# Attention's projection started with the token-by-token unit, between the transposes of the two token tiles

## The chip, the cores and the metric

The kernel runs on one core of one Trainium2 chip. The metric is the device time of one execution in microseconds (us); lower is better. Times are the median of several executions; the rows of the profile come from one profiled execution.

## What is computed

The reference is a network of two blocks, each with two layers, on 256 tokens of width 1024, in float32. Each layer of the first block is a SwiGLU feed-forward, an attention mixer, and a second feed-forward. The change is in the attention mixer, of which this is the part that matters:

```python
proj = h @ w_in                      # h = rms_norm(x), 256 x 1024
q_n, kv_n, gate_n, moba = jnp.split(proj, [...], axis=-1)
# kv_n: k_cmp, v_cmp, k_slc, v_slc, k_win, v_win of two key/value heads
kc = compress(k_cmp, pos_ck, w_ck1, w_ck2)     # gelu(flat(blocks + pos) @ w1) @ w2
vc = compress(v_cmp, pos_cv, w_cv1, w_cv2)
q_rot, k_slc, k_win = (apply_partial_rope(t, cos, sin) for t in (q, k_slc, k_win))
# three branches of scores, softmax and sum, weighted by sigmoid(gate_n);
# beside them eight heads of a second attention (moba), then  @ w_out
```

## The kernel before

The program is written by hand, engine by engine: each phase has a function for SyncE (`sync`, which issues all loads), ScalarE (`scalar`), VectorE (`vector`) and TensorE (`tensor`), and their order is the order of the code. Engines meet only at semaphores. The mixer's phase is `nsa_phase`; it runs twice, once per layer, each time after a feed-forward phase.

**Numbers in two parts.** A float32 product is made of three matmuls of `fp32r` parts (`matmul3`, lines 88 to 90): each operand is split into a high part, which ScalarE writes (`activation ... Copy`), and a low part, which VectorE writes (value minus high). That holds for weights and for activations.

**The norm and the transposes.** The tokens are two tiles of 128 (t = 0, 1). Per tile, ScalarE squares and sums two halves (`norm_scalar`), VectorE adds, inverts and scales (`norm_vector`), TensorE transposes in blocks of four (`turn_block`: block b is half b % 2 of tile b // 2, in bank b), ScalarE copies each block's high part (`turned_high_scalar`) and VectorE makes its low part (`turned_low_vector`). Between the blocks TensorE runs matmuls whose result is not used (`keep_clock(n)`; each of the n is two rows of the trace).

**The ring of weight units.** The projection's weight comes in 12 units of 256 columns, one of them of 280 (the values of two branches and the gate logits). A unit is loaded by SyncE into one of three slots (`Ring.load`), split by ScalarE (`Ring.high`, line 780) and VectorE (`Ring.low`, line 787), and used by its jobs on TensorE. The load of unit n + 3 waits until unit n is split; its high part waits also until unit n's jobs are done. Unit 0 is split while the feed-forward's last matmuls run; units 1 and 2 are split behind the four transposed blocks.

**The jobs.** `jobs` lists 22 of them; the first 12 (`JOBS_FIRST`) stand ahead of attention. A "turned" job computes 128 columns for all 256 tokens (24 matmuls of 256 columns), a "tokens" job computes the 280-column unit for one tile of tokens (24 matmuls of 280 columns). Jobs alternate between banks 0 and 1, so job i waits until ScalarE has copied job i - 2 out (`begin_job`, `copy_job`). A tokens job is copied with a sigmoid for the gates, for which ScalarE loads another function table. Before, the order was: four jobs of compression keys and values (0 to 3), four query jobs (4 to 7), the two keys (8, 9), the two tokens jobs (10, 11).

**Beside the jobs.** After each of jobs 8 to 11 TensorE runs 32 small pairs of matmuls of the compression's hidden layer (`hidden_columns`, line 96); they need VectorE's `key_columns` (16 additions, line 1147), which need the four compression jobs copied. The query and key jobs are rotated on VectorE (`rotate`, four operations). Behind the projection, `repeat_hidden` on VectorE (line 1153) copies the gelu's result, `compressed_kv` on TensorE (line 1387) needs it, and `score_pair` / `mask` start the attention.

**SyncE's order** in the phase: units 0, 1, 2, 3, two small loads, unit 4, the first compression weight (2 MB), unit 5, the second (2 MB), four smaller ones, units 6 and on.

## Time and profile before

| what | value |
|---|---|
| median of 3 runs | 2060.86 us (2060.13 to 2062.85) |
| the profiled execution's own time | 2065.52 us |
| its span | 2063.5 us |
| granted TensorE clock, mean | 0.988 |
| VectorE busy | 66% of the span |
| ScalarE busy | 49% of the span |

The span is what the rows of the trace cover; the execution's own time includes what lies around it. Times in rows count from the span's start. A granted clock of 1.00 is TensorE's 2.4 GHz, 0.50 is 1.2 GHz. Lines are those of the kernel before. In a timeline row, what stands in brackets is the idle time of the engine ahead of the row and what ended it.

### The profile page before, as it was taken

How to read it: one execution, taken by the hardware profiler on the slowest of the kernel's cores; microseconds unless marked ns; L12 is line 12 of the kernel's file. 1: busy time of each engine (PE TensorE's matmuls, PEld its weight loads, DVE VectorE, ACT ScalarE, POOL GpSimd, SP SyncE). 2: the span in 40 equal slices, each digit the busy share in tenths (PEclk: the TensorE clock that was granted, in tenths of full speed). 3: DMA queues.
4: the chain of work that ended last, by engine and by line, in shares of the span. 5: the costliest groups of instructions: out<-in, count | busy, mean ns of one | idle time of the engine just before them, and what ended most of it. 6: DMA issues, size and time to landing. Idle time of an engine off the chain costs nothing. (4 is left out here: it accounts for less than half of the span.)

```text
span 2063.5 us, 41502 instructions
## 1 busy us (share of the span) xinstructions
PE 2007.3 (97%) x17484; PEld 1860.3 (90%) x17484; DVE 1352.2 (66%) x2077; ACT 1005.2 (49%) x1448; POOL 13.0 (1%) x12
## 2 busy tenths in 40 slices
PE   7999999999999999999999999999999999999998
PEld 7999987999999998799989889989998989998997
DVE  7555676754755477675468476668767856577775
ACT  5334466533633355653346444456446534456443
POOL 0000000000000000000000100000000010000000
PEclk9999999999999999999999899999999989999999
DMA  8543732644454373265343424466534423356541
GB/s 313 203 176 113 253 134 85 263 183 190 165 207 189 127 253 112 84 255 202 140 181 139 143 73 144 127 224 246 191 133 174 158 74 119 119 179 254 202 183 52
DMA packets 79877, 348.77 MB, mean 169 GB/s; under 512 B 21233, under 2 KB 30577, under 8 KB 45809
## 3 DMA queue, kind: packets, MB, share of 16 engines
q1 hardware_dynamic: 79728, 346.61, 45.9%
q8 instruction: 116, 1.90, 0.4%
q14 instruction: 33, 0.26, 0.0%
HBM read 345.53 MB, written 1.05 MB: 168 GB/s over the span
## 5 line engine op out<-in xcount | busy, mean ns | idle before, releaser
L88 PE MATMUL bank<-ffn_hT_split,n_split_gate_up 128*128 128x256 f32 x1312 | 364.4, 278 | 2.4 <-DVE ffn_hT_split L212 2.4
L89 PE MATMUL bank<-ffn_hT_split,n_split_gate_up 128*128 128x256 f32 x1312 | 363.8, 277 | 0.0
L90 PE MATMUL bank<-ffn_hT_split,n_split_gate_up 128*128 128x256 f32 x1312 | 363.7, 277 | 0.0
L88 PEld LDWEIGHTS bank<-ffn_hT_split,n_split_gate_up 128*128 128x128 f32 x1312 | 247.2, 188 | 4.3 <-issue 2.8
L89 PEld LDWEIGHTS bank<-ffn_hT_split,n_split_gate_up 128*128 128x128 f32 x1312 | 247.4, 189 | 1.5
L90 PEld LDWEIGHTS bank<-ffn_hT_split,n_split_gate_up 128*128 128x128 f32 x1312 | 247.2, 188 | 0.0
L396 ACT ACTIVATE work<-bank 128x256 f32<-128x256 f32 x88 | 32.9, 383 | 285.2 <-PE bank L90 281.9
L1940 DVE TENSOR_TENSOR mix_parts<-mix_arrived,mix_parts 128x1024 fp32r<-128x1024 f32 x88 | 107.6, 1223 | 92.5 <-ACT mix_parts L1935 92.3
L537 DVE TENSOR_TENSOR work<-bank,work 128x256 f32<-128x256 f32 x88 | 37.2, 423 | 178.8 <-ACT work L396 178.8
L518 DVE TENSOR_TENSOR ffn_split_down<-ffn_arrived_down,ffn_split_down 128x2048 fp32r<-128x2048 f32 x44 | 100.8, 2292 | 81.3 <-ACT ffn_split_down L377 81.3
L472 DVE TENSOR_TENSOR n_split_gate_up<-arrived_gate_up,n_split_gate_up 128x2048 fp32r<-128x2048 f32 x61 | 138.1, 2287 | 11.0 <-ACT n_split_gate_up L367 11.0
L1935 ACT ACTIVATE mix_parts<-mix_arrived 128x1024 fp32r<-128x1024 f32 x88 | 92.9, 1057 | 101.2 <-PE bank L90 95.1
L377 ACT ACTIVATE ffn_split_down<-ffn_arrived_down 128x2048 fp32r<-128x2048 f32 x44 | 84.8, 1928 | 111.7 <-PE bank L90 101.9
L90 PE MATMUL bank<-ffn_split_down,ffn_act_split 128*128 128x512 f32 x352 | 138.8, 394 | 0.0
L89 PE MATMUL bank<-ffn_split_down,ffn_act_split 128*128 128x512 f32 x352 | 138.0, 392 | 0.0
L88 PE MATMUL bank<-ffn_split_down,ffn_act_split 128*128 128x512 f32 x352 | 136.9, 389 | 0.0
L367 ACT ACTIVATE n_split_gate_up<-arrived_gate_up 128x2048 fp32r<-128x2048 f32 x61 | 114.9, 1908 | 0.7 <-DMA arrived_gate_up<-in_ffn 0.6
L787 DVE TENSOR_TENSOR mixer_parts<-mixer_arrived,mixer_parts 128x512 fp32r<-128x512 f32 (+2 forms) x74 | 79.7, 1084 | 52.8 <-ACT mixer_parts L780 52.6
L88 PE MATMUL bank<-normed_T_parts,mix_parts 128*128 128x256 f32 x384 | 110.0, 286 | 0.9 <-DVE mix_parts L1940 0.9
L89 PE MATMUL bank<-normed_T_parts,mix_parts 128*128 128x256 f32 x384 | 106.4, 277 | 0.0
L90 PE MATMUL bank<-normed_T_parts,mix_parts 128*128 128x256 f32 x384 | 106.4, 277 | 0.0
L518 DVE TENSOR_TENSOR conv_ffn_split_down<-onv_ffn_arrived_down,conv_ffn_split_down 128x2048 fp32r<-128x2048 f32 x22 | 50.4, 2291 | 63.4 <-ACT conv_ffn_split_down L377 63.3
(418 smaller groups left out, 5909.4 us busy)
## 6 DMA issues: line engine op xcount, KB each, us to landing
arrived_gate_up<-in_ffn SPq DMA_DIRECT2D x64, 1024.0 KB, 8.4
ffn_arrived_down<-in_ffn SPq DMA_DIRECT2D x44, 1024.0 KB, 4.8
mix_arrived<-in_mix_w SPq DMA_DIRECT2D x88, 512.0 KB, 3.6
rrived_gate_up<-in_conv_ffn SPq DMA_DIRECT2D x32, 1024.0 KB, 6.8
_arrived_gate_up<-in_ffn SPq DMA_DIRECT2D x24, 1024.0 KB, 6.7
mixer_arrived<-in_w_in SPq DMA_DIRECT2D x22, 1024.0 KB, 7.1
onv_ffn_arrived_down<-in_conv_ffn SPq DMA_DIRECT2D x22, 1024.0 KB, 4.9
irst_project_arrived<-in_w_in SPq DMA_DIRECT2D x17, 1024.0 KB, 4.8
```

The costliest lines, as they stand in the source:

```text
L88: pe.matmul(out, lhs[0], rhs[0], start=start, stop=False)
L89: pe.matmul(out, lhs[0], rhs[1], start=False, stop=False)
L90: return pe.matmul(out, lhs[1], rhs[0], start=False, stop=stop)
L367: act.activation(flat(w[part][slot][0]), arrived(part, slot), ACT.Copy).then_inc(s["gu_high"], 1)
L377: act.activation(flat(w[2][slot][0]), arrived(2, slot), ACT.Copy).then_inc(s["down_high"], 1)
L396: act.activation(acts[:, slot, f], c.ps[2 * slot + f][:, 0:S], ACT.Silu).then_inc(s["silu_ready"], 1)
L472: dve.tensor_tensor(flat(low), arrived(part, slot), plain(flat(high)), ALU.subtract).then_inc(s["gu_split"], 1)
L518: dve.tensor_tensor(flat(low), arrived(2, slot), plain(flat(high)), ALU.subtract).then_inc(s["down_split"], 1)
L537: dve.tensor_tensor(value, up, value, ALU.mult).then_inc(s["product_ready"], 1)
L787: last = eng.tensor_tensor(self.parts[slot][1][:, cols], self.arrived[slot][:, cols], plain(self.parts[slot][0][:, cols]), ALU.subtract)
L1935: act.activation(self.parts[n % RING][:, 0], self.arrived[n % RING], ACT.Copy).then_inc(self.s["half_high"], 1)
L1940: dve.tensor_tensor(low, self.arrived[n % RING], plain(high), ALU.subtract).then_inc(self.s["half_split"], 1)
```

## The change

1. `WI_UNITS` is reordered: the 280-column unit becomes unit 0, then come the two compression units, the unit of the two keys, and the two query units. The first slot of the ring is now the wide one; the weight array is laid out in the same order.
2. `jobs` follows: the two tokens jobs are 0 and 1, the compression jobs 2 to 5, the keys 6 and 7, the queries 8 to 11.
3. At the start of the phase TensorE transposes tile 0, runs `keep_clock` of 12, does the first half of job 0 (tile 0), transposes block 2, does the second half of job 0, transposes block 3, runs `keep_clock` of 4, and does job 1 (tile 1). Before, it transposed all four blocks with `keep_clock` of 9, 2 and 4 among them, and then began job 0.
4. ScalarE copies block 0 ahead of tile 1's square root, and VectorE makes block 0's low part ahead of tile 1's reciprocal and block 1's right behind tile 1's scaling.
5. `key_columns` moves from behind step 4 of VectorE's loop to behind step 6, and waits for 6 copied jobs rather than 4.
6. The last two query jobs are rotated behind VectorE's loop, ahead of `repeat_hidden`; `score_pair` waits for as many rotated jobs as each pair needs.

```diff
--- before.py
+++ after.py
@@ -113,7 +113,7 @@
     act.activation(c.stat[:, 7:8], c.eps, ACT.Sqrt)
 
 
-def norm_scalar(act, c, ph, t, before=None):
+def norm_scalar(act, c, ph, t, before=None, between=None):
 
     s, n0 = ph.s, ph.n0
     for half in range(2):
@@ -121,25 +121,29 @@
         if before:
             before.x_ready(act, t, half)
         act.activation(c.h[:, t, cols], c.x[:, t, cols], ACT.Square, accum_out=c.stat[:, n:n + 1]).then_inc(s["sumsq_ready"], 1)
+    if between:
+        between()
     act.wait_ge(s["sum_ready"], n0["sum_ready"] + t + 1)
     act.activation(c.stat[:, 6 + t:7 + t], c.stat[:, 4 + t:5 + t], ACT.Sqrt, bias=c.eps, scale=1.0 / D
                    ).then_inc(s["root_ready"], 1)
 
 
-def inverse_root(dve, c, ph, t):
+def inverse_root(dve, c, ph, t, between=None):
 
     s, n0 = ph.s, ph.n0
     dve.wait_ge(s["sumsq_ready"], n0["sumsq_ready"] + 2 * t + 2)
     dve.tensor_tensor(c.stat[:, 4 + t:5 + t], c.stat[:, 2 * t:2 * t + 1], c.stat[:, 2 * t + 1:2 * t + 2], ALU.add
                       ).then_inc(s["sum_ready"], 1)
+    if between:
+        between()
     dve.wait_ge(s["root_ready"], n0["root_ready"] + t + 1)
     dve.reciprocal(c.stat[:, 4 + t:5 + t], c.stat[:, 6 + t:7 + t]).then_inc(s["rstd_ready"], 1)
     dve.wait_ge(s["rstd_ready"], n0["rstd_ready"] + t + 1)
 
 
-def norm_vector(dve, c, ph, t):
-
-    inverse_root(dve, c, ph, t)
+def norm_vector(dve, c, ph, t, between=None):
+
+    inverse_root(dve, c, ph, t, between)
     if t == 0:
         dve.wait_ge(ph.s["gain_loaded"], ph.n0["gain_loaded"] + 16)
     for half in range(2):
@@ -827,9 +831,9 @@
     c.gates = at("gates", 22560, [P, NT, GATE_COLS])
     c.kc = at("k_cmp", 22608, [P, GROUPS, 16])
     c.vc = at("v_cmp_by_head", 22640, [P, NH, DH])
-    widths = (UNIT, UNIT, W_UNIT)
-    c.units_arrived = [at(f"mixer_arrived{n}", col, [P, w]) for n, (col, w) in enumerate(zip((23152, 25200, 43632), widths))]
-    c.units_parts = [[at(f"mixer_parts{n}_{lo}", col + lo * w, [P, w], F32R)[:] for lo in range(2)] for n, (col, w) in enumerate(zip((27248, 31344, 35440), widths))]
+    widths = (W_UNIT, UNIT, UNIT)
+    c.units_arrived = [at(f"mixer_arrived{n}", col, [P, w]) for n, (col, w) in enumerate(zip((43632, 23152, 25200), widths))]
+    c.units_parts = [[at(f"mixer_parts{n}_{lo}", col + lo * w, [P, w], F32R)[:] for lo in range(2)] for n, (col, w) in enumerate(zip((27248, 31728, 35824), widths))]
     c.cos_part = c.work[:, 0:2 * S].rearrange("p (a n) -> p a n", a=2)
 
     c.kcols = c.h[:].rearrange("p t d -> p (t d)")[:, 0:2 * GROUPS * CJ * N_CMP].rearrange(
@@ -846,7 +850,7 @@
 
 W_IN = 4 * P + 4 * P + 2 * P + 2 * P + GATE_COLS + 3 * Q_COLS
 
-WI_UNITS = [(n * 2 * P, 2 * P) for n in range(5)] + [(10 * P, 2 * P + GATE_COLS)]
+WI_UNITS = [(10 * P, 2 * P + GATE_COLS)] + [(n * 2 * P, 2 * P) for n in (0, 1, 4, 2, 3)]
 WI_UNITS += [(12 * P + GATE_COLS + n * 2 * P, 2 * P) for n in range(6)]
 
 
@@ -901,9 +905,10 @@
                                 "oT_high oT_ready nsa_out nsa_added out_ready residual_done" + NORM_NAMES + RING_NAMES, same_as)
     s, n0 = ph.s, ph.n0
 
-    jobs = [(j // 2, j % 2 * P, "plain", CMP_T + j) for j in range(4)]
-    jobs += [(2 + j // 2, j % 2 * P, "rotate", Q_T + j) for j in range(4)]
-    jobs += [(4, 0, "rotate", KS_T), (4, P, "rotate", KW_T), (5, 0, "tokens", 0), (5, 0, "tokens", 1)]
+    jobs = [(0, 0, "tokens", t) for t in range(NT)]
+    jobs += [(1 + j // 2, j % 2 * P, "plain", CMP_T + j) for j in range(4)]
+    jobs += [(3, 0, "rotate", KS_T), (3, P, "rotate", KW_T)]
+    jobs += [(4 + j // 2, j % 2 * P, "rotate", Q_T + j) for j in range(4)]
     jobs += [(6 + j // 2, j % 2 * P, "rotate", MQ_T + j) for j in range(8)]
     jobs += [(10 + half, 0, "values", 1 + half) for half in range(2)]
     N_IN = len(WI_UNITS)
@@ -1072,9 +1077,10 @@
 
         ring.high(act, 0, width(0))
         root_table(act, c)
-        for t in range(NT):
-            norm_scalar(act, c, ph, t, ph.prev)
-        turned_high_scalar(act, c, FIRST_BANKS, ph, c.hT_parts[:, 0])
+        norm_scalar(act, c, ph, 0, ph.prev)
+        norm_scalar(act, c, ph, 1, ph.prev,
+                    lambda: turned_high_scalar(act, c, FIRST_BANKS, ph, c.hT_parts[:, 0], (0,)))
+        turned_high_scalar(act, c, FIRST_BANKS, ph, c.hT_parts[:, 0], (1, 2, 3))
         for n in range(1, RING):
             ring.high(act, n, width(n))
         for i in range(JOBS_FIRST):
@@ -1134,7 +1140,7 @@
 
         def key_columns():
 
-            dve.wait_ge(s["copied"], n0["copied"] + 4)
+            dve.wait_ge(s["copied"], n0["copied"] + 6)
             dve.wait_ge(s["pos_loaded"], n0["pos_loaded"] + 32)
             for v in range(2):
                 for g in range(GROUPS):
@@ -1255,15 +1261,17 @@
             dve.tensor_tensor(oT_low, o_bank(n)[:].rearrange("p (k n) -> p k n", k=4), plain(oT_high), ALU.subtract
                               ).then_inc(s["oT_ready"], 1)
 
-        turned_low_vector(dve, c, FIRST_BANKS, ph, c.hT_parts[:, 0], c.hT_parts[:, 1])
+        turned_low_vector(dve, c, FIRST_BANKS, ph, c.hT_parts[:, 0], c.hT_parts[:, 1], (2, 3))
         for n in range(1, RING):
             ring.low(dve, n, width(n))
         for i in range(JOBS_FIRST):
             if i - 2 in rotated_jobs:
                 rotate(i - 2)
             low_after(i)
-            if i == 4:
+            if i == 6:
                 key_columns()
+        for i in (JOBS_FIRST - 2, JOBS_FIRST - 1):
+            rotate(i)
         repeat_hidden()
 
         for u in range(N_STEPS):
@@ -1318,8 +1326,8 @@
     def tensor(pe):
         if ph.start:
             ph.start.tables_ready(pe)
-        turn_tensor(pe, c, FIRST_BANKS, ph)
-        pe.wait_ge(s["hT_ready"], n0["hT_ready"] + 3)
+        turn_tile(pe, c, FIRST_BANKS, ph, 0)
+        keep_clock(pe, c, 12)
 
         def begin_job(i):
             pe.wait_ge(s["unit_split"], n0["unit_split"] + jobs[i][0] + 1)
@@ -1330,8 +1338,6 @@
             unit, col, _, _ = jobs[i]
             n_cols = WI_UNITS[unit][1]
             for k in ks:
-                if i == 0 and k == KT // 2:
-                    pe.wait_ge(s["hT_ready"], n0["hT_ready"] + 4)
                 last = matmul3(pe, job_bank(i)[:, 0:S], ring.operand(unit, k * n_cols + col, P), both(c.hT_parts, k),
                                k == 0, k == KT - 1)
             return last
@@ -1340,6 +1346,8 @@
             unit = jobs[i][0]
             n_cols = WI_UNITS[unit][1]
             for k in ks:
+                if i < NT and k % 4 == 0:
+                    pe.wait_ge(s["hT_ready"], n0["hT_ready"] + 2 * t + k // 4 + 1)
                 last = matmul3(pe, job_bank(i)[:, first:first + n_cols], both(c.hT_parts, k, slice(t * P, (t + 1) * P)),
                                ring.operand(unit, k * n_cols, n_cols), k == 0, k == KT - 1)
             return last
@@ -1355,8 +1363,15 @@
             return last
 
         for i in range(JOBS_FIRST):
+            if i == 1:
+                turn_block(pe, c, FIRST_BANKS, ph, 3)
+                keep_clock(pe, c, 4)
             begin_job(i)
-            if jobs[i][2] == "tokens":
+            if i == 0:
+                token_job(0, 0, range(4), 0)
+                turn_block(pe, c, FIRST_BANKS, ph, 2)
+                last = token_job(0, 0, range(4, KT), 0)
+            elif jobs[i][2] == "tokens":
                 last = token_job(i, jobs[i][3], range(KT), 0)
             else:
                 last = turned_job(i, range(KT))
@@ -1417,8 +1432,9 @@
 
         def score_pair(u):
             t = units[u][0]
+            if u < 2 * REP:
+                pe.wait_ge(s["rotated"], n0["rotated"] + 3 + u // 2)
             if u == 0:
-                pe.wait_ge(s["rotated"], n0["rotated"] + 6)
                 pe.wait_ge(s["copied"], n0["copied"] + JOBS_FIRST)
             elif u == MOBA:
                 pe.wait_ge(s["rotated"], n0["rotated"] + len(rotated_jobs))
@@ -1523,8 +1539,13 @@
     def vector_split(dve):
         ring.low(dve, 0, width(0))
 
+    def first_low(dve, b):
+        turned_low_vector(dve, c, FIRST_BANKS, ph, c.hT_parts[:, 0], c.hT_parts[:, 1], (b,))
+
     def vector_norm(dve, t):
-        norm_vector(dve, c, ph, t)
+        norm_vector(dve, c, ph, t, (lambda: first_low(dve, 0)) if t else None)
+        if t:
+            first_low(dve, 1)
 
     def free_gain(sp):
         sp.wait_ge(s["h_ready"], n0["h_ready"] + 2 * NT)
```

What the change moves on two engines, from the order of the built programs (line numbers differ by 4 to 6 between the two).

ScalarE, from the last blocks' copies on, before: rows of line 780 are high parts of units (the number behind `mixer_arrived` is the slot: 83, 84, 85), rows of line 1037 copy two turned jobs.
```order
L125 ACTIVATE norm_stats<-norm_stats,shared_tables 128x1
L123 ACTIVATE normed,norm_stats<-residual 128x512 x2
L125 ACTIVATE norm_stats<-norm_stats,shared_tables 128x1
L204 ACTIVATE mixer_T_parts<-bank 128x4x128 x4
L780 ACTIVATE mixer_parts_0_88<-mixer_arrived_84 128x2048
L780 ACTIVATE mixer_parts_0_90<-mixer_arrived_85 128x2048
L1037 ACTIVATE raw<-bank 128x256 x2
L780 ACTIVATE mixer_parts_0_86<-mixer_arrived_83 128x2048
```
The same place in the changed kernel:
```order
L123 ACTIVATE normed,norm_stats<-residual 128x512 x2
L208 ACTIVATE mixer_T_parts<-bank 128x4x128
L127 ACTIVATE norm_stats<-norm_stats,shared_tables 128x1
L208 ACTIVATE mixer_T_parts<-bank 128x4x128 x3
L784 ACTIVATE mixer_parts_0_88<-mixer_arrived_84 128x2048
L784 ACTIVATE mixer_parts_0_90<-mixer_arrived_85 128x2048
L1044 ACT_TABLE_LOAD
L1044 ACTIVATE gates<-bank 128x24
L1045 ACTIVATE v_tokens<-bank 128x256
L1044 ACTIVATE gates<-bank 128x24
L1045 ACTIVATE v_tokens<-bank 128x256
L784 ACTIVATE mixer_parts_0_86<-mixer_arrived_83 128x2048
```
The table load and the copies of the two tokens jobs (`gates`, `v_tokens`) now stand behind the high parts of units 1 and 2 and ahead of the copies of turned jobs; the first block is copied ahead of the square root.

VectorE in the projection, before: low parts of units 1, 2, 3 and 4, then `key_columns` (line 1147), then unit 5 and the first step of a rotation.
```order
L787 TENSOR_TENSOR mixer_parts_1_89<-mixer_arrived_84,mixer_parts_0_88 128x2048
L787 TENSOR_TENSOR mixer_parts_1_91<-mixer_arrived_85,mixer_parts_0_90 128x2048
L787 TENSOR_TENSOR mixer_parts_1_87<-mixer_arrived_83,mixer_parts_0_86 128x2048
L787 TENSOR_TENSOR mixer_parts_1_89<-mixer_arrived_84,mixer_parts_0_88 128x2048
L1147 TENSOR_TENSOR normed<-raw,pos 64x120 x16
L787 TENSOR_TENSOR mixer_parts_1_91<-mixer_arrived_85,mixer_parts_0_90 128x2240
L1128 STREAM_SHUFFLE rot<-raw 128x256
```
The same place in the changed kernel:
```order
L791 TENSOR_TENSOR mixer_parts_1_89<-mixer_arrived_84,mixer_parts_0_88 128x2048
L791 TENSOR_TENSOR mixer_parts_1_91<-mixer_arrived_85,mixer_parts_0_90 128x2048
L791 TENSOR_TENSOR mixer_parts_1_87<-mixer_arrived_83,mixer_parts_0_86 128x2048
L791 TENSOR_TENSOR mixer_parts_1_89<-mixer_arrived_84,mixer_parts_0_88 128x2048
L791 TENSOR_TENSOR mixer_parts_1_91<-mixer_arrived_85,mixer_parts_0_90 128x2048
L1153 TENSOR_TENSOR normed<-raw,pos 64x120 x16
L791 TENSOR_TENSOR mixer_parts_1_87<-mixer_arrived_83,mixer_parts_0_86 128x2048
L1134 STREAM_SHUFFLE rot<-raw 128x256
```
`key_columns` (line 1153 there) now stands behind the low part of unit 5 (slot 85, the fifth row of line 791).

VectorE at the end of the projection, before: two rotations (lines 1128 to 1133), unit 8's low part, then `repeat_hidden` (the COPY) and the first mask (ISA).
```order
L1128 STREAM_SHUFFLE rot<-raw 128x256
L1129 TENSOR_TENSOR work<-raw,first_tables 128x256
L1131 TENSOR_TENSOR rot<-rot,first_tables 128x256
L1133 TENSOR_TENSOR rot<-rot,work 128x256
L1128 STREAM_SHUFFLE rot<-raw 128x256
L1129 TENSOR_TENSOR work<-raw,first_tables 128x256
L1131 TENSOR_TENSOR rot<-rot,first_tables 128x256
L1133 TENSOR_TENSOR rot<-rot,work 128x256
L787 TENSOR_TENSOR mixer_parts_1_91<-mixer_arrived_85,mixer_parts_0_90 128x2048
L1153 COPY work<-work 128x256
L1248 ISA attention<-bank,first_tables 128x128
```
The same place in the changed kernel:
```order
L791 TENSOR_TENSOR mixer_parts_1_91<-mixer_arrived_85,mixer_parts_0_90 128x2048
L1134 STREAM_SHUFFLE rot<-raw 128x256
L1135 TENSOR_TENSOR work<-raw,first_tables 128x256
L1137 TENSOR_TENSOR rot<-rot,first_tables 128x256
L1139 TENSOR_TENSOR rot<-rot,work 128x256
L1134 STREAM_SHUFFLE rot<-raw 128x256
L1135 TENSOR_TENSOR work<-raw,first_tables 128x256
L1137 TENSOR_TENSOR rot<-rot,first_tables 128x256
L1139 TENSOR_TENSOR rot<-rot,work 128x256
L1159 COPY work<-work 128x256
L1254 ISA attention<-bank,first_tables 128x128
```
Two rotations now stand between unit 8's low part and the COPY.

## Rows read from the trace of the kernel before

**Rows 1.** The page's busy times: engine, busy us, share of span, instructions.
```profile
PE 2007.3 (97%) x17484; PEld 1860.3 (90%) x17484; DVE 1352.2 (66%) x2077; ACT 1005.2 (49%) x1448; POOL 13.0 (1%) x12
```

**Rows 2.** Windows: length, busy us of PE, PEld, DVE, ACT, POOL, then granted clock.
```profile
203.10:245.50 42.40, 42.24 (x544) 41.51 (x544) 30.24 (x54) 19.82 (x23) 0.00 (x0) 1.00 0.81 282
```

**Rows 3.** Timeline of TensorE between the phases: start, length, engine, line, operands.
```profile
197.45 1.04 PE L165 MATMUL bank<-shared_tables,normed 128*128 128x128 f32 x8
198.32 2.17 PE L154 MATMUL bank<-shared_tables 128*128 128x128 f32 x18
...
203.11 0.39 PE L88 MATMUL bank<-mixer_T_parts,mixer_parts 128*128 128x256 f32 x1
```

**Rows 4.** Timeline of ScalarE in the same stretch.
```profile
198.91 0.18 ACT L123 ACTIVATION_READ_ACCUMULATOR normed<-residual 128x1 f32 x1
...
202.23 0.60 ACT L204 ACTIVATE mixer_T_parts<-bank 128x512 fp32r<-128x512 f32 x1 [0.28 <-PE bank L165]
202.72 3.71 ACT L780 ACTIVATE mixer_parts<-mixer_arrived 128x2048 fp32r<-128x2048 f32 x2
...
208.88 0.39 ACT L1037 ACTIVATE raw<-bank 128x256 f32<-128x256 f32 x1 [2.17 <-PE bank L90]
...
211.60 0.39 ACT L1037 ACTIVATE raw<-bank 128x256 f32<-128x256 f32 x1 [0.53 <-PE bank L90]
```

**Rows 5.** Timeline of VectorE from the transposed blocks to unit 5.
```profile
201.18 2.48 DVE L212 TENSOR_TENSOR mixer_T_parts<-bank,mixer_T_parts 128x512 fp32r<-128x512 f32 x4
204.66 4.50 DVE L787 TENSOR_TENSOR mixer_parts<-mixer_arrived,mixer_parts 128x2048 fp32r<-128x2048 f32 x2 [1.01 <-ACT mixer_parts L780]
...
218.75 5.19 DVE L1147 TENSOR_TENSOR normed<-raw,pos 64x120 f32<-64x120 f32 x16
224.13 2.49 DVE L787 TENSOR_TENSOR mixer_parts<-mixer_arrived,mixer_parts 128x2240 fp32r<-128x2240 f32 x1 [0.18 <-ACT mixer_parts L780]
```

**Rows 6.** ScalarE at unit 5 and at the first token job.
```profile
222.01 2.08 ACT L780 ACTIVATE mixer_parts<-mixer_arrived 128x2240 fp32r<-128x2240 f32 x1 [1.87 <-DMA mixer_arrived<-in_w_in]
...
235.85 1.28 ACT L1039 ACT_TABLE_LOAD   x1
...
238.50 0.38 ACT L1040 ACTIVATE v_tokens<-bank 128x256 f32<-128x256 f32 x1
```

**Rows 7.** SyncE's queue: the load of unit 4.
```profile
206.98 0.34 SPq L773 DMA_DIRECT2D mixer_arrived<-in_w_in  x1
```

**Rows 8.** TensorE at the compression's hidden layer and the first scores.
```profile
228.03 2.06 PE L96 MATMUL bank<-normed,w_cmp 128*64 128x30 f32 x64
...
233.03 2.06 PE L96 MATMUL bank<-normed,w_cmp 128*64 128x30 f32 x64
...
243.58 2.06 PE L96 MATMUL bank<-normed,w_cmp 128*64 128x30 f32 x64
245.57 0.49 PE L1429 MATMUL bank<-rot 64*128 64x128 f32 x4
...
248.92 0.53 PE L1387 MATMUL bank<-work,w_cmp 128*128 128x32 f32 x4
```

**Rows 9.** VectorE: two rotations, and the copy for the compressed keys.
```profile
235.59 0.44 DVE L1128 STREAM_SHUFFLE rot<-raw 128x256 f32<-128x256 f32 x1
...
237.06 0.45 DVE L1128 STREAM_SHUFFLE rot<-raw 128x256 f32<-128x256 f32 x1
...
248.19 0.29 DVE L1153 COPY work<-work 128x256 f32<-128x256 f32 x1
```

**Rows 10.** Windows in which TensorE idled, and what followed.
```profile
13.00:15.50 2.50, 0.06 (x1) 0.02 (x1) 2.50 (x5) 2.40 (x2) 0.00 (x0) 1.00 1.03 433
...
1060.00:1063.00 3.00, 0.00 (x0) 0.00 (x0) 1.82 (x6) 2.64 (x7) 0.00 (x0) 1.00 1.05 350
1063.00:1066.00 3.00, 2.92 (x14) 2.92 (x15) 2.56 (x6) 0.73 (x3) 0.00 (x0) 0.53 0.34 142
1066.00:1069.00 3.00, 3.00 (x26) 3.00 (x25) 1.38 (x2) 3.00 (x3) 0.00 (x0) 0.90 0.00 0
```

## The prediction

> **What bounds the kernel now.** First the page's busy times: TensorE is busy for 97% of the span [rows 1]. Such a kernel gets shorter only by TensorE's work or by its waits, so I next looked at how much of either there is where the change works. From the first job to the end of the last hidden-layer matmuls TensorE is busy for 42.24 of 42.40 us at the full clock [rows 2]: 0.16 us of waiting, no more. Ahead of it lies the stretch of the transposes, from 197.45 to the first job's matmul at 203.11, 5.66 us [rows 3]. What it holds: 16 transposes (eight take 198.32 - 197.45 = 0.87, so 1.74 for all) and 15 calls of `keep_clock`, two rows each (18 rows take 2.17, so 0.12 a row, 3.6 for 30). That leaves some 0.3 us of waiting. The other two engines follow TensorE here, and their rows show by how little they are ahead: that is what decides, since the change moves them all. The mixer phase runs twice, and I take the second run to be like the first.
>
> **The first stretch.** The change removes no matmul. It has 16 transposes as before and 16 calls of `keep_clock` for 15. TensorE in the changed order, by the same prices: tile 0's transposes from 197.45 to 198.32, 24 rows of `keep_clock` (2.9) to 201.2, then half of job 0. A tokens job costs 3.29: the hidden-layer matmuls start at 233.03 and, with two tokens jobs and two hidden groups between, at 243.58, so 5.28 for one of each, and a group alone takes 245.57 - 243.58 = 1.99 [rows 8]. Half a job is 1.65: to 202.85. Block 2's transposes (0.44) to 203.3, the second half to 204.95, block 3 (0.44) to 205.4, eight rows of `keep_clock` (0.96) to 206.35, job 1 to 209.65. The operands are there: ScalarE is done with tile 1's squares at about 199.0 [rows 4] and needs 0.6 for block 0, VectorE some 0.62 for its low part (four in 2.48) [rows 5], so 200.3 against 201.2; block 1's low part, behind a scaling that ends at 201.2 before and is now 0.62 later, is done at 202.5 against 203.3. So nothing waits up to here, and the work of jobs 0 and 1 ends at 209.65 where two turned jobs ended before at 203.11 + 2 x 2.72 = 208.55 (2.72 is the distance of two copies, 208.88 and 211.60) [rows 4]. Of the difference of 1.10, 1.14 is that tokens jobs are longer, which is paid back later. The early start itself is worth nothing: what TensorE did not do ahead of job 0 it does behind it.
>
> **ScalarE and VectorE slip by 3.24.** The high parts of units 1 and 2 stand behind the last block's copy, and that block is now transposed behind job 0. The end of `keep_clock` moves from 203.11 to 206.35, and the last copy (202.23) and the high parts (202.72) [rows 4] with it, since the same rows stand between: +3.24. So unit 1's high part starts at 205.96, its low part at 204.66 + 3.24 = 207.90 [rows 5], and it is split at 210.2. ScalarE's two high parts end where the first copy could start, 3.61 on, at 209.57. Now it is job 0's, which needs the other function table: 1.28 for the load [rows 6], 0.1 for the sigmoid's start, 0.38 for the copy: 211.35. Job 2 writes the bank of job 0 and waits for it: 211.4, a stall of 1.75 us. Behind this wait stand all further jobs.
>
> **The hidden layer waits for `key_columns`.** Six jobs of 2.72 from 211.4 end job 8's predecessors at 227.7 and job 8 at 230.45. Its hidden-layer matmuls need `key_columns`, which are now behind unit 5's low part. That has to come from memory: SyncE issued unit 4 when unit 1 was split (206.98) [rows 7], then a 2 MB weight and unit 5, whose high part began at 222.01, released by the DMA after 1.87 of waiting [rows 6]. The queue's whole order is unchanged and starts 3.24 later; unit 5 is 96 KB smaller, for which I take 0.3 off (estimated from its 1.12 MB as the last of 4.3 MB moved in 15 us). So it lands at 224.95; the ends are 222.7, when job 5 is copied and the high part could start at all (2.2 less a phase), and 225.25 without the smaller size. Then 1.94 until the low part may start (204.66 - 202.72), 2.25 for it (half of 4.50), and 5.19 for the additions [rows 4, 5]: 234.35. Before, they started at 218.75, ahead of unit 5 at 224.13, and were done four us before their use at 228.03 [rows 5, 8]. Now the matmuls start at 234.4, a stall of 3.9, and 6.37 later than before. This chain does not hang on TensorE, so it swallows the stall ahead of it: the sum counts 6.37 and not 6.37 + 1.75. The second compression weight, issued behind unit 5, lands before its use at 228.03, so at 231.3 at the latest, inside this wait; load, high parts and rotations of units 6 to 8 slip by about 3.2 as well and have room.
>
> **Behind it, two tokens jobs less.** From 228.03 on TensorE had jobs 9, 10, 11. A turned job with its hidden group takes 233.03 - 228.03 = 5.00, a tokens job 5.28, and there were two: -0.55. The projection ends at 245.57 + 6.37 - 0.55 = 251.4.
>
> **`repeat_hidden` waits behind two rotations.** Before, the copy started at 248.19, was done at 248.48, and TensorE used it at 248.92 [rows 8, 9], a slack of 0.44. Two rotations take 2 x (237.06 - 235.59) = 2.94 [rows 9] and stand now between unit 8's low part, which follows the last job as before, and this copy. So TensorE waits 2.94 - 0.44 = 2.5 there, and all masks start as much later. Nothing behind gives it back, with TensorE at 97%.
>
> **Sum.** +6.37 - 0.55 + 2.5 = +8.3 us a phase, 16.7 for two.
>
> **The clock.** Three waits of 1.75, 3.9 and 2.5 us stand where there were none. Rows of both kinds exist: an idle window of 3 us (1060 to 1063) was followed by 3 us at a granted 0.53, in which 14 matmuls ran where 26 ran in the next 3 at 0.90; an idle 2.45 us at 13.00 was followed by 1.00 [rows 10]. A fall costs 3 x (1 - 14/26) = 1.4 us. I take one for the wait of 3.9 alone, and half of it, as two of the three us go to the hidden layer's 30-column matmuls: 0.7 a phase, bounds 0 and 2.8 (both long waits, in full). The sum becomes +18 us. The Trainium skill, page "TensorE: Matmul & The Clock Gate", section "HAM oscillation — how this bites in real kernels", says that gaps in TensorE's work let its clock fall back and that the price is paid again after each gap; by that rule both long waits would pay, and the sum would be some 3 us higher. The row at 13.00 disagrees for a wait of that size, the row at 1060 agrees.
>
> Against its own time of 2065.52 the profiled execution of the change would take 2083.5; the median of the runs lies 4.7 lower, so the median goes from 2060.86 to **2079**.
>
> **Rivals.** *Only one of the two late waits.* If unit 5's data come early or `key_columns` can run in time, the phase loses at job 2's stall, 211.4 - 208.55 = 2.85, less 0.55, plus 2.5: 4.8 a phase, 2070.5. If instead `repeat_hidden` finds more slack than 0.44 (say that unit 8's high part is earlier, since job 11's copy needs no sigmoid), it is 5.8 a phase: 2072.5. For the first speaks only that loads could be faster with fewer neighbours; the 1.87 us of waiting for the DMA in [rows 6] speak against.
> *Only the copy of job 0 hurts.* 2.3 a phase, 2065.5; it needs both chains above to be wrong.
> *No difference.* If the copy of job 0 does not stand in the way either, the sum of the work is unchanged: 1.10 + 0.24 of longer jobs and one more `keep_clock` less what comes back, within 1 us of 2060.9.
> *Faster.* The jobs start at 201.2 rather than 203.11. Were the transposes of tile 1 and the last `keep_clock` (1.84 us) hidden in waits that TensorE had in the projection anyway, each phase would keep 1.9 us: 2057. It decides from the point where those waits reach 1.84; they are 0.16 [rows 2].
> *Dearer.* The clock falls in all the waits, or the late units delay others: 2086 and more.
>
> **How the numbers follow.** Chances: the forecast (2075 to 2085) 0.60; one late wait (2068 to 2074) 0.20; only job 0's copy 0.08; no difference 0.05; faster 0.02; dearer 0.05. The range from 2067 to 2086 leaves out 0.2: the last four. A difference of 0.2% (4.1 us) is about what a measurement can tell from none. Slower by more than that are the forecast, the single waits, the dearer case and 0.07 of the case of job 0's copy: 0.92. Same: 0.06. Faster: 0.02.
>
> **What the changed profile would show.** In TensorE's timeline: the first 280-column matmuls 3.75 us behind the start of tile 0's transposes; a wait for ScalarE's `v_tokens` copy ahead of job 2; a wait of some 4 us ahead of the first hidden-layer group, released by VectorE's additions; one of some 2.5 us ahead of `compressed_kv`, released by the COPY; and a granted clock under 1.00 behind the second. In ScalarE's, unit 5's high part at about 27.5 us behind the same start, still released by the DMA. I would be wrong if `key_columns` were ready by the end of job 8, that is, if unit 5 landed some 4 us sooner, or if the COPY came less than 0.5 us after TensorE could use it.

## The result, and the profile after

The median of 9 runs of the changed kernel is 2080.98 us (2072.94 to 2090.03), that of 9 runs of the kernel before on the same chip 2062.82 us (2059.47 to 2068.36). The ratio is 1.0095, with a 95% interval of 1.0077 to 1.0112: slower by about 1%, and by more than the 0.2% that can be told from none. The profiled execution took 2082.60 us with a span of 2080.6 us, 17.1 us longer than the span before, at the same mean granted clock of 0.988. Medians here and below are of all executions; in the repeat of experiment 7 one execution, and two of the kernel before beside it, took 3978 to 8743 us, and the ratios leave these three out.

From the page of the changed kernel, first the busy times (answering [rows 1]), then the costliest group that has a wait in the phase: busy, mean ns of one, idle before and its releaser.

```profile
PE 2009.6 (97%) x17488; PEld 1864.1 (90%) x17488; DVE 1352.5 (65%) x2077; ACT 1005.5 (48%) x1448; POOL 13.0 (1%) x12
...
L88 PE MATMUL bank<-mixer_T_parts,mixer_parts 128*128 128x256 f32 x288 | 87.6, 304 | 5.3 <-ACT v_tokens L1045 4.4
```

TensorE's busy time, which counts matmuls at either clock, grew by 2.3 us and the span by 17.1, so nearly all of the difference is waiting; the timelines show 13.9 us of it in the two phases. That the busy time grew so little hides two changes that nearly cancel, as shown below. Of the second row's idle time 4.4 us are two waits, one a phase, for the copy of `v_tokens`, which no row of the kernel before had. The view of waits of TensorE in the first phase (us in total, times, longest us) shows all three new waits:

```profile
PE bank L96 <- DVE normed L1153: 2.5, 1, 2.5
PE bank L1402 <- DVE work L1159: 2.5, 1, 2.5
PE bank L88 <- ACT v_tokens L1045: 2.2, 1, 2.2
```

The timeline of TensorE in the first phase places them. Its first and third rows answer to [rows 3], the last three to [rows 8]:

```profile
198.96 1.03 PE L169 MATMUL bank<-shared_tables,normed 128*128 128x128 f32 x8
199.84 2.84 PE L158 MATMUL bank<-shared_tables 128*128 128x128 f32 x24
202.44 0.38 PE L88 MATMUL bank<-mixer_parts,mixer_T_parts 128*128 128x280 f32 x1
...
212.84 0.36 PE L88 MATMUL bank<-mixer_T_parts,mixer_parts 128*128 128x256 f32 x1 [2.18 <-ACT v_tokens L1045]
...
235.41 3.14 PE L96 MATMUL bank<-normed,w_cmp 128*64 128x30 f32 x64 [2.55 <-DVE normed L1153]
...
255.27 0.49 PE L1445 MATMUL bank<-rot 64*128 64x128 f32 x4
...
261.18 0.60 PE L1402 MATMUL bank<-work,w_cmp 128*128 128x32 f32 x4 [2.48 <-DVE work L1159]
```

ScalarE in the same stretch, for [rows 4, 6]: the high parts of units 1 and 2, the table load, the copy of job 0, and unit 5's high part.

```profile
207.21 3.71 ACT L784 ACTIVATE mixer_parts<-mixer_arrived 128x2048 fp32r<-128x2048 f32 x2
210.93 1.28 ACT L1044 ACT_TABLE_LOAD   x1
...
212.31 0.38 ACT L1045 ACTIVATE v_tokens<-bank 128x256 f32<-128x256 f32 x1
...
226.14 1.92 ACT L784 ACTIVATE mixer_parts<-mixer_arrived 128x2048 fp32r<-128x2048 f32 x1 [1.34 <-DMA mixer_arrived<-in_w_in]
```

VectorE, for [rows 5, 9]: the low parts of units 1 and 2, unit 5's low part, the additions of `key_columns`, and the COPY of `repeat_hidden`.

```profile
209.15 4.49 DVE L791 TENSOR_TENSOR mixer_parts<-mixer_arrived,mixer_parts 128x2048 fp32r<-128x2048 f32 x2 [1.11 <-ACT mixer_parts L784]
...
228.09 2.29 DVE L791 TENSOR_TENSOR mixer_parts<-mixer_arrived,mixer_parts 128x2048 fp32r<-128x2048 f32 x1 [4.81 <-ACT mixer_parts L784]
230.30 5.06 DVE L1153 TENSOR_TENSOR normed<-raw,pos 64x120 f32<-64x120 f32 x16
...
260.75 0.29 DVE L1159 COPY work<-work 128x256 f32<-128x256 f32 x1
```

Every link of the predicted chain stands in these rows. The copy of job 0 runs at 212.31 and job 2 begins at 212.84. Unit 5's data release its high part at 226.14, its low part ends at 230.38, the additions end at 235.36 and the hidden layer begins at 235.41. The COPY starts at 260.75 and `compressed_kv` at 261.18.

TensorE in the second phase: the transposes' start, job 2, the first hidden-layer group, the first scores and `compressed_kv`.

```profile
733.90 1.03 PE L169 MATMUL bank<-shared_tables,normed 128*128 128x128 f32 x8
...
747.75 0.36 PE L88 MATMUL bank<-mixer_T_parts,mixer_parts 128*128 128x256 f32 x1 [2.18 <-ACT v_tokens L1045]
...
770.67 2.61 PE L96 MATMUL bank<-normed,w_cmp 128*64 128x30 f32 x64 [2.02 <-DVE normed L1153]
...
788.95 0.49 PE L1445 MATMUL bank<-rot 64*128 64x128 f32 x4
...
794.86 0.60 PE L1402 MATMUL bank<-work,w_cmp 128*128 128x32 f32 x4 [2.48 <-DVE work L1159]
```

The ends of the phases are marked on SyncE's queue by the load of the next phase's gain vector. First the kernel before, then the changed one:

```profile
164.09 0.42 SPq L105 DMA_DIRECT2D work<-in_norm_mix  x1
296.56 0.43 SPq L105 DMA_DIRECT2D work<-in_norm_ffn  x1
...
684.95 0.42 SPq L105 DMA_DIRECT2D work<-in_norm_mix  x1
817.55 0.43 SPq L105 DMA_DIRECT2D work<-in_norm_ffn  x1
```

```profile
165.60 0.42 SPq L105 DMA_DIRECT2D work<-in_norm_mix  x1
312.07 0.43 SPq L105 DMA_DIRECT2D work<-in_norm_ffn  x1
...
700.47 0.42 SPq L105 DMA_DIRECT2D work<-in_norm_mix  x1
844.13 0.43 SPq L105 DMA_DIRECT2D work<-in_norm_ffn  x1
```

From marker to marker the first mixer phase grew from 132.47 to 146.47 us, by 14.00, and the second from 132.60 to 143.66, by 11.06. Together that is 25.1 us, more than the 17.1 by which the spans differ. The table takes each station as the time since tile 0's transposes began (197.45 and 718.37 before, 198.96 and 733.90 after), and says how much later it is than before; the prediction's are its 6.37, less 0.55, plus 2.5, plus the clock's 0.7.

| station | phase 1, before | after | later by | predicted | later by, phase 2 |
|---|---|---|---|---|---|
| first hidden-layer group | 30.58 | 36.45 | 5.87 | 6.37 | 6.12 |
| first scores | 48.12 | 56.31 | 8.19 | 5.82 | 6.94 |
| `compressed_kv` | 51.47 | 62.22 | 10.75 | 8.32 | 9.49 |
| load that marks the end | 99.11 | 113.11 | 14.00 | 9.0 | 11.05 |

The first row agrees with the prediction; behind it the distance grows where nothing waits. The windows say why (length, busy us of PE, PEld, DVE, ACT, POOL, then the granted clock; they answer to [rows 10]):

```profile
214.80:217.00 2.20, 2.20 (x21) 2.20 (x20) 2.11 (x1) 0.44 (x2) 0.00 (x0) 1.00 1.00 378
236.00:242.60 6.60, 6.60 (x71) 6.54 (x68) 4.72 (x10) 2.08 (x2) 0.00 (x0) 0.50 0.64 232
263.30:270.90 7.60, 7.60 (x40) 6.98 (x38) 2.58 (x11) 1.30 (x7) 0.00 (x0) 0.55 0.00 0
748.00:751.70 3.70, 3.70 (x20) 3.70 (x20) 2.46 (x2) 1.77 (x1) 0.00 (x0) 0.54 0.93 363
772.00:775.80 3.80, 3.80 (x40) 3.74 (x36) 2.92 (x5) 1.12 (x2) 0.00 (x0) 0.56 0.47 192
795.00:799.90 4.90, 4.90 (x29) 4.45 (x29) 2.78 (x13) 1.98 (x9) 0.00 (x0) 0.65 0.15 60
```

Behind job 2's wait the clock held at 1.00 in phase 1 and fell to 0.54 for 3.7 us in phase 2. Behind the hidden layer's wait it was at 0.50 for 6.6 us and at 0.56 for 3.8, behind that for the COPY at 0.55 for 7.6 us and at 0.65 for 4.9. TensorE was busy all through these windows: it worked at 1.2 GHz, not at 2.4.

### The profile page after: what moved, and what is told of

It reads as the page before. It is cut to its first block and busy times, and to the rows that moved or that the text cites. A ratio compares the mean times of both kernels' runs of the same rounds, so it can differ in the third digit from the quotient of the medians.

```text
span 2080.6 us, 41518 instructions
## 1 busy us (share of the span) xinstructions
PE 2009.6 (97%) x17488; PEld 1864.1 (90%) x17488; DVE 1352.5 (65%) x2077; ACT 1005.5 (48%) x1448; POOL 13.0 (1%) x12
## 5 line engine op out<-in xcount | busy, mean ns | idle before, releaser
L476 DVE TENSOR_TENSOR n_split_gate_up<-arrived_gate_up,n_split_gate_up 128x2048 fp32r<-128x2048 f32 x61 | 138.1, 2287 | 11.1 <-ACT n_split_gate_up L371 11.1
L88 PE MATMUL bank<-mixer_T_parts,mixer_parts 128*128 128x256 f32 x288 | 87.6, 304 | 5.3 <-ACT v_tokens L1045 4.4
```

The lines of the kernel that those rows point to most:

```text
L88: pe.matmul(out, lhs[0], rhs[0], start=start, stop=False)
L476: dve.tensor_tensor(flat(low), arrived(part, slot), plain(flat(high)), ALU.subtract).then_inc(s["gu_split"], 1)
```

## The experiments

Experiments 1 to 4 were run together, then 5 to 7 with the first half of 8, then 7 again with the second half of 8 and 9. Experiments 5 and 9 edit the kernel before, the others the changed one. Each ratio is to the kernel before, run in turn with it; its median was 2062.46, 2062.11 and 2063.56 us in the three groups.

**1. `key_columns` ahead of unit 5's low part.** They need jobs 2 to 5 and nothing of unit 5.

```diff
             if i - 2 in rotated_jobs:
                 rotate(i - 2)
-            low_after(i)
-            if i == 6:
+            if i == 5:
                 key_columns()
+            low_after(i)
```

> The changed kernel, with VectorE's key_columns one step earlier, ahead of unit 5's low part instead of behind it. Theory (three waits, the second is the late key_columns): the additions end some 5 us earlier, the hidden layer's first group no longer waits for them but at most a few tenths for the second compression weight; it starts 3 to 3.5 us earlier in each phase, and the fall of the granted clock behind it is gone. Together 7 to 12 us less than the changed kernel's 2081, so 2069 to 2074. Rival (the loads are late, and the additions only stand where TensorE would wait for data anyway): the wait stays, put down to the weight's DMA, and the time stays within 3 us of 2081.

Measured: 2074.06 us, ratio 1.0057 (1.0039 to 1.0075). The wait for the additions is gone; the one for `v_tokens` (2.2 us) and this one stayed:

```profile
PE bank L1402 <- DVE work L1159: 2.5, 1, 2.5
```

So that wait was the position of `key_columns` on VectorE, and what stood ahead of them was unit 5. About 7 us of the 18 to 19 went with it.

**2. The last two rotations ahead of the last unit's low part**, so that `repeat_hidden` is not behind them.

```diff
             if i - 2 in rotated_jobs:
                 rotate(i - 2)
+            if i == JOBS_FIRST - 1:
+                rotate(i - 1)
+                rotate(i)
             low_after(i)
             ...
-        for i in (JOBS_FIRST - 2, JOBS_FIRST - 1):
-            rotate(i)
         repeat_hidden()
```

> The changed kernel, with the last two rotations on VectorE ahead of unit 8's low part, in a time in which VectorE waited for ScalarE, instead of between it and the copy that compressed_kv needs. Theory: the wait of 2.5 us ahead of compressed_kv goes in each phase, and with it the second fall of the clock: 5 us at least, up to 11, so 2070 to 2076. Rival (the masks and the exponent's function table would hold the attention up as long, so the wait only moves): TensorE waits for a mask or an exponential instead, time within 2 us of 2081.

Measured: 2073.36 us, ratio 1.0062 (1.0043 to 1.0081). The wait for the COPY is gone; the one for `v_tokens` (2.2 us) and this one are there:

```profile
PE bank L96 <- DVE normed L1153: 3.3, 1, 3.3
```

Both phases grew by 8.2 us over the kernel before instead of 14.0 and 11.1.

**3. Both edits.**

> The changed kernel with both moves. Theory: what is left is the wait for job 0's copy, 1.75 to 2.2 us a phase, less 0.55 for the shorter jobs: 2065 to 2069, some 0.2% above the kernel before. If the two waits fed each other (one clock fall for both), the gain is less than the sum of the two single moves. Rival (starting with the tokens jobs is itself dearer, in TensorE's work): it stays above 2072.

Measured: 2064.40 us, ratio 1.0012 (1.0001 to 1.0023). What is left in the first phase:

```profile
PE bank L88 <- ACT v_tokens L1045: 2.2, 1, 2.2
PE bank L1403 <- DVE work L1159: 1.2, 1, 1.2
```

The two edits bring back about 17 of the 18 to 19 us, some 2 us more than the two alone add up to, which the intervals allow for. The time is a little under the 2065 to 2069 expected. In the profile the phases are still 6.4 and 3.3 us longer than before: the wait for job 0's copy is still there, a wait of 1.2 us for the COPY has come up in the first phase, and the clock fell once in each phase, behind the COPY's wait in the first (0.50 from 257.0 to 263.6) and behind job 2's in the second.

**4. All waits kept, the clock held.** Ten calls of `keep_clock` (20 rows) fill the hidden layer's wait and the one for the COPY. The ends of the waits are set by VectorE and should not move by this: TensorE does something in them.

```diff
             last.then_inc(s["projected"], 1)
+            if i == 8:
+                keep_clock(pe, c, 10)
             if i >= 8:
                 last = hidden_columns((i - 8) // 2, i % 2)
...
             pe.wait_ge(s["wc2_loaded"], n0["wc2_loaded"] + 64)
+            keep_clock(pe, c, 10)
             pe.wait_ge(s["repeated"], n0["repeated"] + 1)
```

> The changed kernel, with 10 matmuls whose result is not used ahead of the wait for key_columns and 10 ahead of the wait for the copied hidden layer (2.4 us each, no longer than the waits). No wait is removed. Theory (the waits cost 7.8 us a phase, and the fall of the clock behind them another 3 to 6): the granted clock stays at 1.00 behind both, and 6 to 10 us of the 18 go: 2071 to 2075. Rival (the clock costs nothing beyond what later waits would have taken): within 2 us of 2081.

Measured: 2072.49 us, ratio 1.0063 (1.0039 to 1.0087). TensorE's rows at the two places in the first phase:

```profile
233.40 2.39 PE L158 MATMUL bank<-shared_tables 128*128 128x128 f32 x20
235.72 2.06 PE L96 MATMUL bank<-normed,w_cmp 128*64 128x30 f32 x64
...
255.83 2.39 PE L158 MATMUL bank<-shared_tables 128*128 128x128 f32 x20
258.38 0.63 PE L1405 MATMUL bank<-work,w_cmp 128*128 128x32 f32 x4 [0.15 <-DVE work L1159]
```

The 64 hidden-layer matmuls take 2.06 us again, not 3.14, and the windows behind both places have a granted clock of 1.00. Only a fall behind job 2's wait was left, in this execution in phase 1 (0.56 for 3.8 us) and not in phase 2. By it job 8 ended late in phase 1, and the filling outlasted the additions there by 0.9 us (they end at 234.79), so this run gives the clock's share a little too small. The phases grew by 8.9 and 7.7. By the ratios (1.0095 less 1.0063) 6.6 us of the loss, by the two phases of the profiles 8.5 (25.1 less 16.6), were the clock's answer to the two later waits, and not the waits. Here the Trainium skill, page "TensorE: Matmul & The Clock Gate", section "HAM oscillation — how this bites in real kernels", says that the clock falls back in gaps of TensorE's work and that the price is paid again after each; its example is of longer gaps than these, and that both long waits would pay by it was my reading. The windows of the changed kernel agree for both late waits in both phases, and disagree for job 2's wait in phase 1, behind which the clock held at 1.00.

**5. The kernel before, with late `key_columns` alone.** The same displacement without the new job order: the additions behind unit 5's low part, which VectorE makes in step 5 (`i == 5`).

```diff
-            if i == 4:
+            if i == 5:
                 key_columns()
```

> The kernel before, with key_columns moved behind unit 5's low part alone (one step later on VectorE); nothing else of the change. Theory: the additions start at 226.4 and end at 231.5, TensorE waits for them at 228.0, 3.5 us in each phase, and the clock may fall behind it: 7 to 12 us slower than the kernel before, 2069.5 to 2074.5. Rival (in the order before, something else hides it): within 2 us of 2062.5.

Measured: 2072.94 us, ratio 1.0059 (1.0041 to 1.0077), phases longer by 6.4 and 5.2 us. Its wait in the first phase:

```profile
PE bank L96 <- DVE normed L1147: 3.6, 1, 3.6
```

This one move makes a wait of 3.6 us (3.8 in phase 2), about the 3.5 expected, and costs nearly 11 us in the median.

**6. Unit 1 split earlier**: its high part behind block 1's copy, job 0's copy (with its table load) ahead of unit 2's, and the low parts to match.

```diff
-        turned_high_scalar(act, c, FIRST_BANKS, ph, c.hT_parts[:, 0], (1, 2, 3))
-        for n in range(1, RING):
-            ring.high(act, n, width(n))
+        turned_high_scalar(act, c, FIRST_BANKS, ph, c.hT_parts[:, 0], (1,))
+        ring.high(act, 1, width(1))
+        turned_high_scalar(act, c, FIRST_BANKS, ph, c.hT_parts[:, 0], (2, 3))
         for i in range(JOBS_FIRST):
             copy_job(i)
+            if i == 0:
+                ring.high(act, 2, width(2))
...
+        ring.low(dve, 1, width(1))
         turned_low_vector(dve, c, FIRST_BANKS, ph, c.hT_parts[:, 0], c.hT_parts[:, 1], (2, 3))
-        for n in range(1, RING):
-            ring.low(dve, n, width(n))
+        ring.low(dve, 2, width(2))
```

> The changed kernel, with unit 1 split behind tile 0's blocks, in idle time of ScalarE (3.0 us) and VectorE, and job 0 copied ahead of unit 2's high part. key_columns and the rotations stay late. Theory: job 2 starts without a wait (2.2 us less), unit 1 is split and unit 4 loaded some 5 us earlier, so unit 5 lands earlier, and the wait for key_columns falls from 2.5 to under 1.5 us: 4 us and more a phase, 8 to 12 in all, 2069 to 2073. Rival (the order of VectorE alone makes that wait): the wait for the additions grows by what TensorE gains, and the time stays within 3 us of 2081.

Measured: 2072.02 us, ratio 1.0049 (1.0031 to 1.0066). The wait for `v_tokens` is gone in both phases. In the first, counted from tile 0's transposes (198.09 in this run), the additions start at 27.06 rather than 31.34 and the hidden layer at 32.22 rather than 36.45; unit 5's high part no longer waits for its data, and the hidden layer waits 1.5 us. But the phases grew by 14.3 and 6.5 us in the profile. Its windows behind the wait of 2.48 us for the COPY in phase 1, and behind that of 1.5 us for the additions in phase 2:

```profile
255.00:278.70 23.70, 23.70 (x120) 21.73 (x119) 9.55 (x37) 6.23 (x24) 0.00 (x0) 0.50 0.01 2
767.00:771.00 4.00, 4.00 (x38) 3.94 (x37) 3.91 (x8) 0.29 (x2) 0.00 (x0) 0.60 0.42 123
```

One wait of 2.48 us cost 23.7 us at half the clock, that is 11.9 us of TensorE's work. The same wait was followed by 7.6 us in the changed kernel, and by 3.3 us at 0.50 in this kernel's second phase.

**7. All three edits (1, 2 and 6).**

> The changed kernel with all three: key_columns and the rotations ahead, unit 1 split early. Theory: all three waits are gone, TensorE's work is that of the kernel before plus one call of keep_clock a phase: 2060 to 2064, no difference to the kernel before that can be measured. Rival (the tokens jobs first cost something of themselves): 2 us or more above the kernel before.

Measured: 2053.61 us, ratio 0.9960 (0.9947 to 0.9973). The only wait left in the first phase is one that the kernel before has as well:

```profile
PE bank L88 <- ACT raw L1042: 0.3, 1, 0.3
```

The phases are 0.59 and 0.64 us shorter than before. The time is 6 us under the lower end of what was expected. Run again with the last group:

> The same kernel as g3, once more, since 2053.6 lies 9 us under the kernel before and its two phases were only 1.2 us shorter in the profile. If the rest is chance in where the clock falls in the stretches that the change does not touch, this comes back at 2057 to 2063. If it belongs to this order, it comes back at 2052 to 2055.

Measured: 2055.49 us, ratio 0.9959 (0.9947 to 0.9970). The version beats the kernel before by 0.4% or 8 us in both groups, and so the changed one by more. Of these only 0.59 + 0.64 = 1.2 us are in the two phases that the edits touch. The same windows in two later stretches that no edit touches, first of the kernel before, then of this one:

```profile
1150.00:1215.00 65.00, 59.23 (x630) 52.98 (x630) 34.99 (x57) 27.45 (x42) 6.18 (x3) 0.89 0.25 79
1650.00:1710.00 60.00, 54.99 (x591) 48.54 (x589) 33.92 (x55) 23.52 (x37) 6.17 (x3) 0.89 0.24 78
```

```profile
1150.00:1215.00 65.00, 59.19 (x728) 53.69 (x727) 38.88 (x65) 29.17 (x45) 6.19 (x3) 1.00 0.26 83
1650.00:1710.00 60.00, 54.04 (x713) 48.14 (x714) 37.08 (x65) 25.10 (x44) 6.18 (x3) 1.00 0.24 78
```

In its profiled execution the kernel before ran them at 0.89. The timed runs go the same way: the median granted clock of the kernel before was 0.992, that of this version 0.996.

**8. The same with less filling.** Nine calls of `keep_clock` for 12, and none for the 4 ahead of job 1.

```diff
-        keep_clock(pe, c, 12)
+        keep_clock(pe, c, 9)
...
                 turn_block(pe, c, FIRST_BANKS, ph, 3)
-                keep_clock(pe, c, 4)
```

> As g3, with keep_clock of 9 for 12 ahead of job 0 and none for 4 ahead of job 1. Theory: in this order useful matmuls stand between the transposes, so the filling is not needed; 7 calls a phase at 0.24 us are 1.7 us, 3.4 in all: 2057 to 2060, 0.1 to 0.2% under the kernel before. Rival (the operands are then not there and TensorE waits instead, or the clock falls): the time of g3.

Measured: 2058.26 us, ratio 0.9983 (0.9970 to 0.9996). The phases are 1.0 and 1.1 us shorter than before, more so than in 7, and the kernel is 4.7 us slower than in 7. With nine for 12 and the four kept:

> As g3, with keep_clock of 9 for 12 ahead of job 0 and the 4 ahead of job 1 kept: 0.7 us less of TensorE's filling in each phase. By work alone 1.4 us under g3. If what the stretches behind lose depends on when in the program they come, as g4's 2058.3 against g3's 2053.6 suggests, it can come out several us above g3.

Measured: 2060.72 us, ratio 0.9991 (0.9980 to 1.0003), 5.2 us above 7 run beside it, with both phases 1.0 us shorter than before.

**9. The kernel before with more filling**: four more calls of `keep_clock` ahead of job 0 in each phase, 2 x 8 x 0.12 = 1.9 us of work more.

```diff
         turn_tensor(pe, c, FIRST_BANKS, ph)
+        keep_clock(pe, c, 4)
```

> A control: the kernel before with 4 more calls of keep_clock ahead of job 0 in each phase, 0.96 us each, 1.9 us in all, nothing else. By work alone 1.9 us above the kernel before, 0.1%. If the time moves by more than 3 us, or down, then such shifts alone change what the clock costs later in the program, and differences of a few us between these kernels are not to be put down to the phase.

Measured: 2057.75 us, ratio 0.9988 (0.9973 to 1.0002), at a median granted clock of 0.995. The phases grew by 0.46 and 0.43 us only. More work did not make the kernel slower; whether it is faster the interval leaves open. By the expectation, differences of a few us between these kernels are then not to be put down to the phase, and most of the gain of 7 is such a difference.

## Why the prediction was right, and where it was not

**The first stretch: right.** The first 280-column matmul came 202.44 - 198.96 = 3.48 us behind the transposes (3.75 predicted), and job 2 at 13.88 behind them (13.95). The earlier start brought nothing.

**Job 2's wait: right, 2.18 us for 1.75.** The ends of table load and copy were within 0.2 of the forecast, and TensorE was done with job 1 0.5 sooner than forecast. Experiment 6 removed the wait by making unit 1's high part earlier and moving the copy ahead of unit 2's, which shows that ScalarE's order was the cause.

**`key_columns`: right in kind, the size of the stall too large.** Unit 5's high part began 27.18 us behind the transposes (27.5 predicted), still released by the DMA, and the hidden layer was 5.87 and 6.12 us later (6.37). The stall was 2.55 and 2.02 us and not 3.9, for two reasons: job 8 ended 33.90 behind the transposes and not 33.0, as the seven jobs ahead took 2.86 us each where I had used the distance of two copies, 2.72; and the additions ended 0.5 earlier. Since the chain does not hang on TensorE, only the second of these changed the sum. Experiments 1 and 5 show the cause from both sides.

**`repeat_hidden`: right.** 2.48 us for 2.5 in both phases; experiment 2 removed it by the order of VectorE's queue alone.

**The sum without the clock: right.** 16.7 us predicted. From the table, less the clock's part between first hidden group and first scores (8.19 - 5.87 + 0.55 = 2.87 and 6.94 - 6.12 + 0.55 = 1.37), `compressed_kv` was later by 7.88 and 8.12 us: 16.0.

**The clock: the mis-sized term.** I took one fall for the 3.9 us wait alone, half of it, 0.7 a phase and 1.4 in all, with 2.8 a phase as the upper bound, and no fall for waits of 2.5 us or less, by the row at 13.00 in [rows 10]. Measured in the phases: 2.87 + 3.25 in the first (3.25 from 14.00 - 10.75) and 1.37 + 1.56 in the second, together 9.1 us, and a fall behind job 2's wait in phase 2 besides, which the next wait swallowed. The first phase's 6.1 lies far above my bound, the second's 2.9 at it. Experiment 4 gives 6.6 to 8.5 us for the same. Three errors stood behind it: I took the length of one fall (3 us at 1060) for that of all, and it can be 3.7 to 7.6 us in this kernel; I let one row acquit all waits of its size (behind it the clock did hold, at 1.00 from 15.50 to 20.00); and I took the hidden layer's small matmuls for free of the clock, where 64 of them took 3.14 and 2.61 us for 2.06.

**Why the time was still right.** In the profiled pair the two phases grew by 25.1 us, the span only by 17.1: the other 8 came back in stretches that the change does not touch. They hold the two windows of experiment 7, which the kernel before had run at 0.89; the same work, 22 to 27 us later in the changed kernel, ran at 0.97 and 1.00. My 18 thus met 18.2 in the medians with the clock's term nearly 8 us too small, and without the gain elsewhere, for which I had no term. The forecast's waits and its sign stand on the experiments; that its total came within 2 us of 2080.98 is in part luck.

**The rivals.** *Only one of the two late waits* is experiment 1 or 2: 9.6 and 11.6 us above the kernel before by my working, 11.6 and 10.9 measured, but it did not happen by itself. *Only job 0's copy* is experiment 3: 4.6 us above by my working, 1.9 measured. *Faster* fell by what it said itself: TensorE had no waits in which the moved transposes could hide. It took all three waits to be undone, and then each phase kept 0.6 us, not 1.9. *Dearer* had the right mechanism, the clock falling behind nearly every wait, but the median stayed 5 us under its 2086.

**What stays open.** Why the time of later stretches depends on the order here. Experiment 7 takes 1.2 us out of the phases and is 8 us faster; experiment 8 takes out another 1 and gives 5 us of it back; experiment 9 puts 1.9 us of work in and is not slower. The median granted clocks go along (0.996 and 0.995 for 7, 0.992 for both of 8, 0.995 for 9, 0.992 to 0.993 for the kernel before).

The traces show one such place. From the load of the final norm's gain to the next gain's load SyncE's marks are 306.0 to 308.4 us apart in the kernel before, experiment 5 and both of experiment 8, and 300.2 to 302.1 in the other nine executions. In the middle of it TensorE needs the weight `in_sg_w_s`. SyncE's load behind that one and TensorE's wait, first in the kernel before, then in experiment 7:

```profile
1176.24 1.76 SPq L2383 DMA_DIRECT2D low_rank<-in_sg_ln_b  x1
1179.41 1.11 PE L2937 MATMUL bank<-shared_tables,inner 128*128 128x128 f32 x4 [1.65 <-DMA inner<-in_sg_w_s]
...
1175.92 0.42 SPq L2407 DMA_DIRECT2D low_rank<-in_sg_ln_b  x1
1177.83 0.66 PE L2961 MATMUL bank<-shared_tables,inner 128*128 128x128 f32 x4 [1.26 <-DMA inner<-in_sg_w_s]
```

The row of SyncE's queue is 1.76 to 2.39 us long in the four, 0.42 in the nine; TensorE waits 1.65 to 3.15 us for the weight in the four, 1.26 at most in the nine; and the mean granted clock of the 28 us around it is 0.70 to 0.88 in the four, 0.94 to 1.00 in the nine. So there a load comes later and the clock is low for longer. Whether the one causes the other was not tested (in the kernel before the clock is low already when this wait begins), nor what delays the load. Each is one execution.

## What to carry to other kernels

Before a job is moved ahead, write down for each engine what now stands in front of its copy and in front of what the next stage waits for: here three places in two queues, where something stood behind work that it does not need, cost 1%, and the same new job order with those three places put right was the fastest version measured (by 0.4%, most of it far from the edits). Where TensorE is busy for 97% of the span, count the clock behind a new wait too (here 9.1 us behind 13.9 us of waits); where the wait can't be removed, work that holds the clock inside it brought most of that back in experiment 4. A gain smaller than one fall of the clock has to be measured on the whole kernel, more than once, since it can be lost or doubled in stretches far from the edit.

## What was not expected of the hardware

The time at the lower clock behind a wait had no fixed length. Waits of 2.48 us for the same COPY were followed by 7.6 us (0.55), 4.9 us (0.65) and, in experiment 6, 23.7 us (0.50) and 3.3 us (0.50), with TensorE busy all through; a wait of 1.2 us in experiment 3 was followed by seven us at 0.51, beginning 2.4 us later, and the wait of 2.18 us ahead of job 2 in the changed kernel by no fall in phase 1 and by 3.7 us at 0.54 in phase 2. So the length of a wait alone did not say what it cost.
